# A two-layer transformer kernel in which the conditioning matrix is read and summed one stage ahead of its use

## What is computed

```python
cond = jax.nn.silu(c)
h = x                                               # 256 tokens x 1024
for l in range(DEPTH):                              # DEPTH = 2
    mod = (cond @ ada_w[l] + ada_b[l]).reshape(bsz, N_MOD, 1, dm)
    sh1, sc1, g1, sh2, sc2, g2, sh3, sc3, g3 = [mod[:, i] for i in range(N_MOD)]
    u = rms_norm(h, norm_g[l, 0]) * (1.0 + sc1) + sh1
    h = h + 0.5 * g1 * swiglu(u, ffn_w_in[l, 0], ffn_w_out[l, 0])
    u = rms_norm(h, norm_g[l, 1]) * (1.0 + sc2) + sh2
    h = h + g2 * hybrid_mixer(u, ...)               # three kinds of attention behind one projection
    u = rms_norm(h, norm_g[l, 2]) * (1.0 + sc3) + sh3
    h = h + 0.5 * g3 * swiglu(u, ffn_w_in[l, 1], ffn_w_out[l, 1])
```

## Time and profile before

| | us |
|---|---|
| time, median of 3 runs | 1284.91 (1284.45 to 1288.61) |
| span of the profiled execution, first to last instruction | 1282.7 |
| PE busy in the span | 1211.6 |
| DVE busy | 882.3 |
| ACT busy | 458.7 |
| granted TensorE clock, mean over the span | 0.953 of full speed |
| moved from HBM | 248.6 MB, 195 GB/s over the span |

### The profile page before, as it was taken

One profiled execution on the slowest core, in us unless ns is written; L12 is line 12 of the kernel. 1 busy time (PEld: TensorE's weight loads), 2 busy tenths in 40 slices (PEclk: granted clock), 3 DMA queues, 4 the chain that ended last, 5 costly groups with the idle time before them and its releaser, 6 DMA issues.

```text
span 1282.7 us, 21042 instructions
## 1 busy us (share of the span) xinstructions
PE 1211.6 (94%) x8503; PEld 1061.4 (83%) x8511; DVE 882.3 (69%) x1576; ACT 458.7 (36%) x722; POOL 33.9 (3%) x30
## 2 busy tenths in 40 slices
PE   1599999999989999999999999999998999999998
PEld 1499999966457679999989999996655767999998
DVE  6799997555775677777559999745586666555553
ACT  1343333221144454433335333322113444444332
POOL 6300000000000000000000000000000000000000
PEclk7699999998969989999999999999986998999999
DMA  8999997226203328887666999631720241655540
GB/s 339 353 329 380 365 366 239 60 88 143 98 1 132 123 94 289 265 272 259 206 230 224 374 362 370 237 100 35 196 99 1 86 138 40 212 170 175 196 131 34
DMA packets 147438, 250.48 MB, mean 195 GB/s; under 512 B 7718, under 2 KB 126132, under 8 KB 142260
## 3 DMA queue, kind: packets, MB, share of 16 engines
q1 hardware_dynamic: 146676, 248.38, 56.8%
q10 hardware_dynamic: 704, 1.30, 0.3%
HBM read 248.62 MB, written 1.05 MB: 195 GB/s over the span
## 4 chain that ended last, share of the span: by engine, by line
PE 89%; DVE 7%; DMA 2%; issue 1%; ACT 1%; SPq 0%; ACTq 0%; DVEq 0%
PE ps L487 38%; PE ps L576 10%; PE ps L514 8%; PE ps L515 8%; PE ps L516 8%; DMA ada<-in_ada_w_dram 2%; PE ps L617 2%; PE ps L457 2%; PE ps L596 2%; PE ps L605 2%; PE ps L677 2%; PE ps L595 1%; PE ps L585 1%; PE ps L450 1%; DVE sq L1203 1%; DVE wl L1186 1%
## 5 line engine op out<-in xcount | busy, mean ns | idle before, releaser
L1186 DVE TENSOR_TENSOR wl<-wide,wh 128x2048 fp32r<-128x2048 f32 x88 | 201.6, 2291 | 15.8 <-ACT wh L837 15.7
L863 ACT ACTIVATE fs<-ps 128x256 f32<-128x256 f32 x88 | 33.7, 383 | 469.6 <-PE ps L487 465.0
L514 PE MATMUL ps<-fh,th 128*128 128x256 f32 x704 | 200.6, 285 | 0.4 <-DVE fl L1243 0.4
L515 PE MATMUL ps<-fl,th 128*128 128x256 f32 x704 | 199.2, 283 | 0.0
L516 PE MATMUL ps<-fh,tl 128*128 128x256 f32 x704 | 199.2, 283 | 0.0
L487 PE MATMUL ps<-uh,wh 128*128 128x256 f32 x1344 | 189.1, 283 | 3.3 <-DVE wl L1186 3.3
L487 PE MATMUL ps<-ul,wh 128*128 128x256 f32 x1344 | 188.7, 283 | 0.0
L487 PE MATMUL ps<-uh,wl 128*128 128x256 f32 x1344 | 188.7, 283 | 0.0
L487 PEld LDWEIGHTS ps<-uh,wh 128*128 128x128 f32 x1344 | 173.3, 192 | 4.1 <-DVE wl L1186 4.1
L487 PEld LDWEIGHTS ps<-uh,wl 128*128 128x128 f32 x1344 | 173.4, 192 | 0.0
L487 PEld LDWEIGHTS ps<-ul,wh 128*128 128x128 f32 x1344 | 173.4, 192 | 0.0
(11 more groups left out here) (249 smaller groups left out, 1364.2 us busy)
## 6 DMA issues: line engine op xcount, KB each, us to landing
wide<-in_ffn_w_in_dram SPq DMA_DIRECT2D x88, 1024.0 KB, 8.4
ada<-in_ada_w_dram SPq DMA_DIRECT2D x38, 1536.0 KB, 7.2
tall<-in_ffn_w_out_dram SPq DMA_DIRECT2D x44, 1024.0 KB, 5.1
wide<-in_w_in_dram SPq DMA_DIRECT2D x14, 1024.0 KB, 6.1
ada<-in_ada_w_dram SPq DMA_DIRECT2D x16, 768.0 KB, 4.5
tall<-in_w_out_dram SPq DMA_DIRECT2D x8, 1024.0 KB, 7.9
wide<-in_c_cmp_w_dram SPq DMA_DIRECT2D x4, 1024.0 KB, 11.5
wide<-in_w_in_dram SPq DMA_DIRECT2D x4, 832.0 KB, 6.2
```

The source lines that it names most:

```text
L514: mm(y[:, d, :], th[:, a, cols], hi, start=False, stop=False, skip_group_check=True)
L515: mm(y[:, d, :], th[:, a, cols], lo, start=False, stop=False, skip_group_check=True)
L863: A(fs[:, m % 2, :], ps[:, m % 2, 0:SEQ], ACT.Silu).then_inc(silu_ready, 1)
L1186: tt(wl[:, a, :, :, :].rearrange("p e k n -> p (e k) n"), raw, wh[:, a, :, :, :].rearrange("p e k n -> p (e k) n").bitcast(F32), ALU.subtr ...
```

## The change

The conditioning vectors are loaded in another division. Ahead of the first stage only shift and scale of the first norm are made, from eight pieces of 1 MB, of which two go to the `wide` slots and two to the `tall` slots; four rounds follow. `ffn(l, 0)` takes the next four vectors in 16 pieces of 1 MB (8 rounds). The third norm's shift and scale move into the mixer: eight pieces of 1 MB, summed by DVE into a new buffer `accm`, four before it prepares lat and four after; PE turns them in four new entries `mr0` to `mr3` of `AUX` behind hid, and DVE sums these behind gate. `ffn(l, 1)` takes its own gate and, in layer 0, the next layer's first shift and scale: eight pieces of 0.5 MB and eight of 1 MB (6 rounds); in layer 1 the eight of 0.5 MB alone (2 rounds). In a feed-forward stage the vectors are finished during the last tiles and not after the residual.

The first norm's squares, sums and reciprocal root are done after the third of the eight first pieces; ten `keep_warm` products that PE had in this norm stand behind the four rounds. In the first stage ACT rounds the first two weight tiles after the shift and no longer before it, and DVE does its eight `ul` parts before the first tile's rest. Clearing `acc` by ACT (L859) is gone, since the first piece is written by a plain multiplication. All hardware loops, over layers and over tiles, are written out.

```diff
+AUX[AUX.index(("qa", "act")):AUX.index(("qa", "act"))] = [(f"mr{r}", "dve") for r in range(4)]
...
-ADA_PRO = KD - 2
-ADA_L = 4 * KD
-PRO_BANKS = (0, 1, 4, 5, 6, 7)
+PRO_BANKS = (0, 1, 2, 3)
+ADAW = 2 * DM
+ADA_F0, ADA_MIX, ADA_F1 = 2 * KD, KD, 2 * KD
+ADA_L = ADA_F0 + ADA_MIX + ADA_F1
+ADA_ROUNDS = (8, 6)
...
+        def ada_at(l, phase, n):
+
+            return KD - 4 + l * ADA_L + (0, ADA_F0, ADA_F0 + ADA_MIX)[phase] + n
...
+            def ada_mix(l, k):
+                fill_ada(ada_at(l, 1, k), ADAW, ada_w[l, k * P:(k + 1) * P, 6 * DM:8 * DM])
...
+            first = (wide[:, 0, 0:ADAW], wide[:, 1, 0:ADAW], tall[:, 0, :], tall[:, 1, :])
             for k in range(KD):
-                src = ada_w[0, k * P:(k + 1) * P, 0:3 * DM]
-                if k in (2, 3):
-                    sp.dma_start(wide[:, k - 2, 0:3 * DM], src).then_inc(first_in[k - 2], 16)
+                src = ada_w[0, k * P:(k + 1) * P, 0:ADAW]
+                if 2 <= k < 6:
+                    sp.dma_start(first[k - 2], src).then_inc(first_in[k - 2], 16)
                 else:
-                    fill_ada(n, n % 2, 3 * DM, src)
-                    n += 1
+                    fill_ada(k if k < 2 else k - 4, ADAW, src)
...
                 n = WIDE_M
                 fill_wide(l, n, [cols(n, 0, 512, 720, 416), cols(n, 208, 720, 928, 416)],
                           (wide_used, (2 * l + 1) * NPAIR + 1))
+                for k in range(2):
+                    ada_mix(l, k)
                 n += 1
...
+                for k in range(4, 6):
+                    ada_mix(l, k)
...
                 fill_wide(l, n, [(w1[r:r + 64, :, :], w1_src[r:r + 64, :, :]) for r in (0, 64)],
                           (proj, projected(l, F_CMPIN)))
+                for k in range(6, KD):
+                    ada_mix(l, k)
...
+                pe.wait_ge(accm_ready, l + 1)
+                for r in range(4):
+                    turn(l, f"mr{r}", [(v * P, accm[:, (4 * r + v) * P:(4 * r + v + 1) * P]) for v in range(4)])
...
+            norm_stats(0, 0)
             pe.wait_ge(acc_ready, 1)
-            pe.wait_ge(h_ready, KD)
-            for r in range(6):
+            for r in range(4):
                 for v in range(4):
-                    i = tr(ps[:, PRO_BANKS[r], v * P:(v + 1) * P], acc[:, (4 * r + v) * P:(4 * r + v + 1) * P], ident)
+                    i = tr(ps[:, 4 + r, v * P:(v + 1) * P], acc[:, (4 * r + v) * P:(4 * r + v + 1) * P], ident)
                 i.then_inc(mod_ps, 1)
-            with pe.Fori(0, DEPTH - 1) as l:
+            keep_warm(10)
+            pe.wait_ge(mod_red, 4)
...
+            squares(0, 0)
+            act.wait_ge(trig_in, 1)
+            A(trg[:, 0:192], trg[:, 0:192], ACT.Sin).then_inc(trig, 1)
...
+                if l == 0 and f == 0:
+                    round_wide(l, f, n0, 0)
+                    round_wide(l, f, n0, 1)
...
+            for k in range(3):
+                first_piece(k)
...
+            rstd_rows(0, 0)
+            for k in range(3, KD):
+                first_piece(k)
...
+            norm_rows(0, 0)
...
-                width = 3 * DM if f == 0 else 1536
...
+            def ada_sum(l, phase, n, k, part, width):
+
+                at_ = ada_at(l, phase, n)
+                dve.wait_ge(ada_in[at_ % 2], ada_landed(l, phase, n))
+                piece = ada[:, at_ % 2, 0:width]
+                if k == 0:
+                    ts(part, piece, cond[:, 0:1], None, ALU.mult).then_inc(ada_used, 1)
+                else:
+                    stt(part, piece, cond[:, k:k + 1], part, ALU.mult, ALU.add).then_inc(ada_used, 1)
+                dve.wait_ge(ada_used, at_ + 1)
...
+                for k in range(4):
+                    mix_ada(k)
...
+                for k in range(4, KD):
+                    mix_ada(k)
+                V.memset(small[:, 1:2], 0.0).then_inc(accm_ready, 1)
...
+                for r in range(4):
+                    aux_wait(l, f"mr{r}")
+                    sum_parts(r, aux_bank(f"mr{r}"), msum).then_inc(aux_dve, 1)
+                dve.wait_ge(*aux_done("mr3", l))
+                unit(msum[:, 0:2 * KD], adab(l, 2), ng(l, 2), 2).then_inc(mod_ready, 1)
...
-            with dve.Fori(0, DEPTH - 1) as l:
+            for l in range(DEPTH - 1):
```

More of the change, by code:

```diff
@@ L410, in layer @@
                           (wide_used, (2 * l + 1) * NPAIR + 2))
+                for k in range(2, 4):
+                    ada_mix(l, k)
                 n += 1
@@ L540, in ffn @@
             def ffn(l, f, last=False):
-                norm_stats(l, 2 * f)
+                if l or f:
+                    norm_stats(l, 2 * f)
                 open_y()
                 gate_up_first(l, f)
-                with pe.Fori(0, KD // 2) as i:
+                for i in range(KD // 2):
                     for q in range(4):
@@ L552, in ffn @@
                     for r in range(2 * (m - 2 * KD), 2 * (m - 2 * KD) + 2):
-                        if r < 12 - 6 * f and not last:
+                        if r < (2 if last else ADA_ROUNDS[f]):
                             sum_parts(l, f, r)
@@ L854, in ffn @@
                 shift(l, 2 * f, uh)
-                if not last:
-                    width = (2 - f) * 3 * DM
-                    nc.scalar.copy(acc[:, 0:width], zb[:, 0:1].broadcast_to([P, width])).then_inc(acc_zero, 1)
+                if l == 0 and f == 0:
+                    round_wide(l, f, n0, 0)
+                    round_wide(l, f, n0, 1)
                 def tile(m, i=0):
@@ L868, in tile @@
                         round_wide(l, f, n0, m + 2, i)
-                with act.Fori(0, KD // 2) as i:
+                for i in range(KD // 2):
                     for q in range(4):
@@ L985, in _ @@
             act.wait_ge(tables, 1)
-            with act.Fori(0, DEPTH - 1) as l:
+            for l in range(DEPTH - 1):
                 ffn(l, 0)
@@ L1145, in _, with first_piece @@
             link(i)
-            n = 0
-            for k in range(KD):
-                if k in (2, 3):
+            first = (wide[:, 0, 0:ADAW], wide[:, 1, 0:ADAW], tall[:, 0, :], tall[:, 1, :])
+            def first_piece(k):
+                if 2 <= k < 6:
                     dve.wait_ge(first_in[k - 2], 16)
-                    piece = wide[:, k - 2, 0:3 * DM]
+                    piece = first[k - 2]
                 else:
+                    n = k if k < 2 else k - 4
                     dve.wait_ge(ada_in[n % 2], 16 * (n // 2 + 1))
@@ L1223, in ffn @@
                 n0, m0 = (WIDE_A, TALL_A) if f == 0 else (WIDE_B, TALL_B)
-                norm(l, j)
-                width = 3 * DM if f == 0 else 1536
-                if f == 0:
+                if l or f:
+                    norm(l, j)
+                if l and f == 0:
                     rest_wide(l, 0, 0)
```

194 lines of the change are left out of this document (104 added, 90 removed).

## The result

| | before | changed |
|---|---|---|
| median of 20 runs each, us | 1286.66 (1283.23 to 1288.61) | 1290.58 (1287.69 to 1294.03) |
| ratio, 95% interval | | 1.0033 (1.0025 to 1.0041) |
| span of the profiled execution | 1282.7 | 1292.1 |
| PE busy, DVE busy | 1211.6, 882.3 | 1219.8, 881.5 |

The change costs 3.9 us (3.2 to 5.3 by the interval) where the prediction had 1.9 us less. The two profiled executions lie 9.4 us apart, 5.5 more than the medians: that of before is one of its shorter ones and that of the changed kernel one of its longer, so places are read from the traces here and sizes from the medians.

The account below looks back on a forecast made before the run. PE, busy 94% of the span, was taken as the bound, with holes at the start. Start -15.5, rounds -3.5 and +0.9, mixers +16.2 sum to -1.9, so 1284.9 becomes 1283.0 us; range 1276.0 to 1291.0.

Parts of the forecast that it names:

- each wait that was named as its sign: Mixer: DVE idle for `ada` transfers, some 10 us in sum; PE waiting for DVE at `mr2` and kc; hid without wait.
- The mixer, forecast +8.1: Each layer's mixer: pieces 6 and 7 land behind w1, delaying qa, the rounds, kc and F_CK; 8.1 us more, twice.
- I allow 1 behind: Mixer, piece 7: it lands 1 us after its moving ends, at 310.9, and its pass ends at 313.2.
- The floor of 5.0: Mixer: even with early pieces, the rounds behind hid cost 5.0 us each, if piece 7 is used before 309.
- rival 2: Mixer: pieces behind w1 come early, each mixer loses only 5.0 us; 1276.8 us in all; chance 0.31.
- The start, forecast -15.5: Ahead of the second tile: fewer conditioning pieces and rounds let it start at 53.5 instead of 69.03, 15.5 us less.
- it took 4.3, so 23.3: Start: the first norm's chain takes 4.3 us, as before, behind the third piece's sum at 19.0, ending at 23.3.
- The low clock that the range had 4.2 us for: Start, PE's two groups of products: at granted clock 0.50 they take 4.2 us more, 1287.2 us in all; chance 0.05.
- Eight rounds for twelve: Each `ffn(l, 0)`: two pairs of rounds fewer on PE, 2 x 0.87 us; 3.5 us less over both layers.
- The last stage: `ffn(1, 1)`: a pair of rounds where it had none, 0.9 us more.
- The written-out loops: All stages: writing out the loops was put at nothing, since the tile crossing a loop's edge takes 8.64 us like every other.
- rival 3: Mixer: w1 comes too late for hid, with 4 us of delay in each mixer 1291.0 us in all; chance 0.17.

Follow-up runs that it names:

- passes_no_transfers: Changed kernel with the mixer's eight pieces not loaded, DVE's eight passes run over what lies in the slots, rounds kept: 1279.93 us, 0.9946.
- the corners: Four kernels with the changed start: mixer pieces and rounds both absent (1269.70 us), pieces only (1284.88), rounds only (1280.18), both, the changed kernel (1290.58).
- neither: Changed kernel without pieces or rounds in the mixer, eight rounds in `ffn(l, 0)`, third norm's vectors built from other sums: 1269.70 us, 0.9867.
- start_alone: Changed kernel without pieces or rounds in the mixer; third norm's vectors made in `ffn(l, 0)` again, 16 pieces of 1.5 MB, 12 rounds: 1271.94 us, 0.9897.
- the eight: The traces of the eight kernels whose start is the changed one's, itself among them; second tile at 54.2 to 58.6 us.
- warm_before_first_group: start_alone with 16 more products on zeros on PE between the rounds' sums and the first group: 1271.17 us, 0.9884.
- spread_and_warm: start_alone with reciprocal root behind the fifth piece, DVE's spread wait moved to its reader, and 14 and 15 products on zeros in PE's holes: 1267.71 us, 0.9854.
- w1_behind: Changed kernel with pieces 6 and 7 ahead of w1 in SP's list instead of behind it: 1303.65 us, 1.0125.
- rounds_alone: Changed kernel without the mixer's eight loads and eight passes; the rounds turn and sum a buffer of zeros: 1280.18 us, 0.9955.

## Why the prediction was wrong

The mechanism was as forecast, start against mixers, and so was each wait that was named as its sign: DVE for transfers of `ada`, PE for gate at `mr2` and for kc, and none of hid. The signs that were times missed: the second tile at 56.4 and not 53 to 54, the memset at 38.7 and not near 36, qa's preparation 10.6 us later behind F_A than before and not 8. Two terms of the sum were mis-sized, both to the same side, and the sum changed its sign.

**The mixer, forecast +8.1, measured +10.4 each** (20.9 / 2 by the medians; 10.4 and 11.1 in the trace). The step that failed is "I allow 1 behind". In the changed kernel's time, 12.3 us less than before at F_LAT, the forecast had w1 moved by 292.7, piece 7 moved by 297.6, landed by 298.6 and its pass ended at 300.9. Windows of the changed kernel over the stretch:

```profile
282.00:292.00 10.00, 10.00 (x25) 4.50 (x24) 4.50 (x2) 0.58 (x1) 0.00 (x0) 1.00 1.20 208
...
294.00:296.00 2.00, 2.00 (x6) 0.76 (x4) 0.00 (x0) 0.98 (x2) 0.00 (x0) 1.00 0.99 376
296.00:297.00 1.00, 1.00 (x7) 0.72 (x6) 0.00 (x0) 0.66 (x2) 0.00 (x0) 1.00 1.00 418
297.00:298.00 1.00, 1.00 (x11) 1.00 (x10) 0.00 (x0) 0.00 (x0) 0.00 (x0) 1.00 1.00 410
298.00:299.00 1.00, 1.00 (x11) 1.00 (x10) 0.78 (x1) 0.00 (x0) 0.00 (x0) 1.00 0.98 349
```

w1 moves at 208 GB/s until about 293, the pieces at 410 to 418 until about 298, and what comes behind them (F_CQ's weights) at 349. The forecast had 297.6, so up to 0.5 us is the moving. But DVE has piece 7 only at 300.8, and its pass ends at 303.2: 2.3 late, of which the landing is the larger part, 2.6 to 2.8 where 1 was allowed. The earlier trace rows had 5.1 us from issue to landing for 2.5 of moving; the other 2.6 lies, here at least, behind the moving and not half ahead of it. The Trainium skill says as much ("DMA: Bandwidth & Descriptors", Anatomy of one DMA, written for GpSimd's path, where these transfers are SyncE's): a fixed part of about 2.0 us, most of it the wait for the last byte's receipt; the trace agrees in kind and has 2.6 to 2.8. Weighed in the prediction, its 2.0 us in place of the 1 would have brought the mixer to about 9, by an estimate from that page's figure; the measured 2.6 gives 9.7. The chain behind it then ran as the prediction wrote it, gate, `mr2`, qb, kc, F_CK, and carried the 2.3 us through. That the pieces cost by this wait and not by DVE's passes is shown by passes_no_transfers: without the transfers they cost nothing. It leaves w1 with no pieces ahead of it or behind it as well, so it doesn't tell the 2.6 us of landing from the time that w1 takes to move; that split is not shown by an experiment and rests on the windows above.

The floor of 5.0, for rounds behind hid with early pieces, was right within what the corners can tell: 5.2 without pieces (5.6 by the ratios), and the same with passes but no transfers. So rival 2's price held and only its condition didn't. What the Trainium skill states ("DMA: Bandwidth & Descriptors", Specifications) would have w1, in runs of 512 bytes, move at line rate; the trace has 208 GB/s, and disagrees again.

**The start, forecast -15.5.** The corner with neither addition is 16.4 us under the before of its group (17.1 by the ratio, 15.2 to 19.2), where -15.5 - 3.5 + 0.9 gives 18.1: the times alone don't tell these apart, the traces do. In the changed kernel's own trace the second tile is 12.6 us sooner, in start_alone's 14.4, and none of the eight has more than 14.8. The step is "it took 4.3, so 23.3": the norm's chain was moved to a place where its input wasn't ready in every execution and where GpSimd was at work beside it. The wait for PE's short products was 2.3 us in the trace of the changed kernel and nothing in start_alone's, where these took 4.59 us instead of 6.99; that alone makes the start's gain move by 2 us from one execution to another. Five of the eight traces have the 6.99, the other three 4.59 to 5.25. The chain itself was longer too: two of its instructions took 0.56 and 0.57 us where the same ones took 0.16 before. GpSimd was busy beside them (3.58 us of 20 to 24); whether that is the reason was not tried. From the memset to the second tile the forecast had 17.8 us (35.7 to 53.5), the trace 17.7. The low clock that the range had 4.2 us for did come, in the first group (3.51 us for 2.08), but DVE's first rest was ready only at 52.12, so it cost 0.5.

**The smaller terms.** Eight rounds for twelve gave 1.4 and 1.3 us in the tiles of the two `ffn(l, 0)` instead of 1.74; where a round had stood, PE now has a short hole for `fl`, 0.22 us at 241.71. What makes the rest of the difference was not tried. The last stage cost +0.9, as forecast. The written-out loops cost nothing and gave nothing, shown by the kernel before with its loops written out.

**The sum again**, by the medians: the start with the rounds and the last stage -16.4, the two mixers +20.9, +4.5; measured +3.9. Of the 5.8 us between forecast and result the mixers hold 4.7 and the start, with its rounds and the last stage, 1.7; that is 0.6 too much, because the before of that corner's group was 0.6 lower (1286.07 for 1286.66). The time itself is 7.6 us over 1283.0: these 5.8 and the 1.75 by which the three runs that the forecast started from lay under the median of twenty. The range held the time, at its upper end, which is luck as much as foresight. Its upper end had been drawn for rival 3, a late w1, which did not happen: hid had no wait.

## What to carry to other kernels

A load is worth moving ahead to a stage only if its consumer there is not in the chain that this stage waits for: here 16.4 us were gained in one place and 20.9 paid in two, and the same change without that part runs at 0.9897 of before. A pass that fits into an engine's idle time costs nothing only if its data are there in that time, so price the last transfer up to its landing, 2.6 us behind its moving, and ask which engine is idle when it lands. Work on PE's queue behind a long block is a wait for whoever needs its result, however small it is: four rounds of 0.9 us behind hid cost 5.2 a mixer.

## What the runs showed of the hardware

The granted clock of a window says little on PE's pace at the start. The sixteen transposes took 3.52 us in the changed kernel, and 3.68 in warm_before_first_group; their windows give 1.00 for the one (38.8 to 42.3 by itself too) and 0.50 for the other:

```profile
36.00:42.00 6.00, 3.17 (x15) 3.17 (x16) 4.14 (x6) 0.00 (x0) 0.00 (x0) 1.00 1.06 373
```

```profile
36.00:42.00 6.00, 4.47 (x18) 3.87 (x20) 4.06 (x8) 0.00 (x0) 1.09 (x1) 0.50 1.07 375
```

In spread_and_warm, where PE was kept busy ahead of them, they took 1.97, again at 1.00. The sums' products of one column took 4.59 to 6.99 us ahead of the first stage for the same 32, run by run. In w1_behind hid took 13.83 us in both layers, behind a wait, at a granted clock of 0.50, where the changed kernel had 9.63 and 10.35. But rounds_alone had 12.06 in layer 0 without a wait, passes_no_transfers 12.02 and neither 11.52, so the wait is not the whole of it, and what drew the clock down there stays open.
